# A third row slot lends its place to a head's weights while the expert lookups of a layer begin

## The reference, cut to what matters

```
q   = (xt @ w_q).reshape(T, 8, 2, 128)              # T = 256 tokens, 8 heads
sc  = einsum('thcd,hckd->thck', q, sub_keys)        # scores on 2 x 128 keys per head
...                                                 # two top-16, their sums, a top-16 of those
idx, gate = 16 experts of each head, softmax(top_s)
hid = gelu(einsum('tkd,td->tk', u[idx], x))         # 128 experts of each token
out = einsum('tk,tkd->td', gate * hid, v[idx])
h   = h + out
g   = sigmoid(rms_norm_2(h, ple_norm[i]) @ ple_gate[i])
h   = h + g * (p[i] @ ple_proj[i])
```

## Time and profile before

| | |
|---|---|
| median of three runs | 2379.18 us |
| the profiled execution, its own time | 2381.23 us |
| its span, from the first to the last instruction | 2379.1 us |
| gathers of the first PEER layer, first and last issue | 765.2 and 1415.9 us |
| PE, DVE, ACT, POOL busy | 88%, 73%, 33%, 27% |
| moved by the 16 DMA engines | 726.83 MB, mean 306 GB/s |

### The profile page before, as it was taken

The page is one execution under the profiler, slowest core; times in us unless marked ns, Lnnn a source line. Parts: engine busy times, 40 slices in busy tenths (PEclk is TensorE's granted clock), DMA queues, the critical chain, the costliest instruction groups (busy, mean ns, idle before and its releaser), DMA issues. The chain is left out here.

```text
span 2379.1 us, 26606 instructions
## 1 busy us (share of the span) xinstructions
PE 2101.1 (88%) x9124; PEld 1362.4 (57%) x9124; DVE 1741.4 (73%) x3737; ACT 788.2 (33%) x1479; POOL 633.5 (27%) x520
## 2 busy tenths in 40 slices
PE   8999999999999989887877778999898987777777
PEld 8998889989877544432322226988554532222224
DVE  6555764557766888888787876656888887878786
ACT  4334653346574221211211116344322121211114
POOL 0000000000101444444544440000454554444440
PEclk9999999999999999999999999999999999999999
DMA  7554325554326999999999995535999999999994
GB/s 264 182 183 170 142 103 181 184 187 154 140 89 236 402 420 420 419 419 419 392 420 420 418 391 207 206 142 197 359 419 420 419 419 420 402 420 419 405 420 192
DMA packets 101354, 726.83 MB, mean 306 GB/s; under 512 B 11632, under 2 KB 11888, under 8 KB 13424
## 3 DMA queue, kind: packets, MB, share of 16 engines
q0 software_dynamic: 74016, 539.00, 55.1%
q1 hardware_dynamic: 25200, 181.41, 20.9%
q10 hardware_dynamic: 2016, 4.89, 0.6%
HBM read 724.21 MB, written 1.05 MB: 305 GB/s over the span
## 5 line engine op out<-in xcount | busy, mean ns | idle before, releaser
L2074 PE MATMUL bank<-arena 128*128 128x512 f32 (+4 forms) x2416 | 1072.4, 575 | 235.2 <-DVE arena L1953 230.1
L725 POOL DMA_INDIRECT arena<-in_uv,expert x512 | 622.7, 1216 | 1015.0 <-PE bank L2074 552.3
L2074 PEld LDWEIGHTS bank<-arena 128*128 128x128 f32 (+2 forms) x2416 | 411.6, 193 | 806.0 <-DVE arena L1953 526.2
L2003 DVE SCALAR_TENSOR_TENSOR arena<-arena,xn 128x1024 f32<-128x1024 f32 x512 | 625.9, 1222 | 103.6 <-DMA arena<-in_uv,expert 100.8
L1321 DVE TENSOR_TENSOR lw_rounded<-lw,w_hi 128x2048 fp32r<-128x2048 f32 x153 | 352.8, 2307 | 200.4 <-ACT w_hi L778 197.3
L1216 ACT ACTIVATE act_h<-hid 128x1 f32<-128x1 f32 x512 | 103.8, 203 | 1052.3 <-DVE arena L2003 1051.9
L2074 PE MATMUL bank<-xT_hi,w_hi 128*128 128x256 f32 x1320 | 413.2, 313 | 6.6 <-DVE xT_lo L1366 4.9
L778 ACT ACTIVATE w_hi<-lw 128x2048 fp32r<-128x2048 f32 (+1 forms) x173 | 313.0, 1816 | 237.9 <-PE bank L2074 226.8
L2074 PE MATMUL bank<-xT_lo,w_hi 128*128 128x256 f32 x1320 | 373.5, 283 | 0.0
L2074 PE MATMUL bank<-xT_hi,lw_rounded 128*128 128x256 f32 x1256 | 355.6, 283 | 0.0
L1953 DVE TENSOR_SCALAR arena<-consts,act_h,weight 128x128 f32<-128x128 f32 x512 | 191.2, 373 | 127.0 <-ACT act_h L1216 119.3
(11 more groups left out here) (262 smaller groups left out, 1583.9 us busy)
## 6 DMA issues: line engine op xcount, KB each, us to landing
lw<-in_units SPq DMA_DIRECT2D x165, 1024.0 KB, 4.8
arena<-in_uv,expert POOLq DMA_INDIRECT x512, 14.0
arena<-in_units SPq DMA_DIRECT2D x4, 1024.0 KB, 8.0
wide<-in_wide POOLq DMA_DIRECT2D x2, 1024.0 KB, 8.9
gain<-in_gains ACTq DMA_DIRECT2D x4, 512.0 KB, 9.0
wide<-in_units SPq DMA_DIRECT2D x2, 1024.0 KB, 7.2
h<-in_x SPq DMA_DIRECT2D x2, 512.0 KB, 4.6
arena<-in_ret_consts ACTq DMA_DIRECT2D x1, 1024.0 KB, 4.8
```

Source lines behind the costliest of these rows:

```text
L725: nc.gpsimd.indirect_dma_start(out=rows_uv[:, slot, :], out_offset=None, in_=table, in_offset=bass.IndirectOffsetOnAxis(ap=expert[par][:, ...
L2003: V.scalar_tensor_tensor(rows_uv[:, slot, 0:D], rows_uv[:, slot, 0:D], 1.0, xn[:, tile, :], ALU.mult, ALU.mult, accum_out=hid[par][:, k:k ...
L2074: return nc.tensor.matmul(o, lhsT, rhs, start=start, stop=stop, **more)
```

## The change

Three blocks instead of two hold a head's weights at first: head 4's unit, `head + 5`, goes to a third block of `rows_uv` (block 2 in the first layer, 6 in the second), and that block joins as a slot at gather 43. A layer starts with five slots, has six from gather 16, seven from 29 and eight from 43. The ring's place that held `head + 5` is free for `head + 9`, the projection's unit, which is now loaded right behind `head + 2` and the third block, and no longer after head 4. The third block is loaded behind the wait for `head - 2`, since in the second layer other data lies there before.

```
-UNIT_BLOCKS = ((0, 1), (4, 5))
-JOINS_AT = (16, 29)
+UNIT_BLOCKS = ((0, 1, 2), (4, 5, 6))
+JOINS_AT = (16, 29, 43)
...
-        block_loaded = [sem(f"block_loaded{i}") for i in range(2)]
+        block_loaded = [sem(f"block_loaded{i}") for i in range(len(JOINS_AT))]
...
+                def load_block(i):
+                    sp.dma_start(rows_uv[:, UNIT_BLOCKS[layer][i], :], units_d[head + 3 + i]).then_inc(block_loaded[i], 16)
+
                 for i in range(2):
-                    sp.dma_start(rows_uv[:, UNIT_BLOCKS[layer][i], :], units_d[head + 3 + i]).then_inc(block_loaded[i], 16)
-
-                for u, before in ((head + 2, head - 2), (head + 5, head - 3), (head + 7, head - 1), (head + 6, head + 2), (head + 8, head + 1),
-                                  (head + 9, head + 5)):
+                    load_block(i)
+
+                for u, before in ((head + 2, head - 2), (head + 9, head - 3), (head + 7, head - 1), (head + 6, head + 2), (head + 8, head + 1)):
                     sp.wait_ge(lw_used, before + 1)
                     load_unit(u, u % RING)
+                    if u == head + 2:
+
+                        load_block(2)
```

More of the change, by code:

```diff
@@ L207 @@
         FILLED[layer].append(fills[block])
-BLOCK_OF = {first + 3 + i: UNIT_BLOCKS[layer][i] for layer, first in enumerate((A_PEER0, A_PEER1)) for i in range(2)}
+BLOCK_OF = {first + 3 + i: UNIT_BLOCKS[layer][i] for layer, first in enumerate((A_PEER0, A_PEER1)) for i in range(len(JOINS_AT))}
 LOADS = {u: sum(v not in WHOLE and v not in BLOCK_OF for v in range(u % RING, u + 1, RING)) for u in range(UNITS)}
```

## The result

The changed kernel takes 2382.81 us (median of 20 runs, 2379.91 to 2387.80) against 2378.96 us of the kernel before in the same series. The ratio of the runs is 1.0019, 95% interval [1.0013, 1.0026]: 4.5 us slower. The prediction had +0.6 us, "the same" at 0.87, and a range up to 2383.0. The time lies in the range, and the loss is under the 4.8 us that the prediction called the same. But the interval of ±1.5 us tells it from no change: a small, real loss was forecast as nearly nothing. Two later series of the same kernel gave 1.0010 and 1.0008; weighted by their intervals the three give 1.0014 [1.0009, 1.0018], or +3.3 us, and that is the number to be explained.

The account below looks back on a forecast made before the run. Bounds: an idle gap, a start paced by DVE, PE and slot release, then a long stretch of DMA bytes. First layer 0.0 plus second +0.7, taken as +0.6 on 2379.18, gave 2379.8 us; range 2376.6 to 2383.0.

Parts of the forecast that it names:

- The projection's unit leaves the full stretch: Moving this 1 MB load out of the DMA-bound part, behind gather 36, saves 2.50 us a layer, 5.0 in all.
- the gap: About 5 us before a layer's first gather, DMA share 0.04 in the first; claimed to hide the moved load free.
- rival D: The moved load runs past the first gather, costing up to 2.5 us a layer: 2384.8 us at most; chance 0.03.
- Five slots instead of six for gathers 5 to 15: At each layer's start, late landings delay gather 15: +2.1 to +2.6 us in the first layer, +3.2 in the second.
- the walk: Gathers 5 to 15 followed slot by slot, issue plus latency (7.5 or 8.1 us) against old dots, giving gather 15's delay.
- Gather 5: no cost: First layer's start: issued at 784.12, landing at 791.6, while its dot stood behind others until 792.9 anyway.
- Six slots in place of seven ... cost nothing: Gathers 16 to 28, likewise seven for eight up to 42: queueing covers the lost slot, by 0.2 us at its thinnest.
- The signs: Profile checks: SP's sends, gather issues, DVE waits, about 350 GB/s, gather 17's dot 2 to 3 us later; DMA gaps refute.
- B: The start absorbs the lost slot and the full gain of 5.0 us arrives: 2374.2 us; chance 0.05.
- C: Five and also six slots starve at gathers 8 to 28: +3.5 us a layer, 2386.2 us; chance 0.07.
- The price of the Trainium skill: Fixed 2.0 us plus bytes over 436 GB/s: 4.4 us a gather, making five slots ample, 2374.2 us; prediction rejected it.

Follow-up runs that it names:

- small_proj: Kernel before, loading only 64 of 2048 columns of the projection's unit: 2375.02 us, ratio 0.9983.
- slots_only: Changed kernel, but with the projection's unit loaded last, at its old place behind head 4: 2387.21 us, ratio 1.0033.
- again: The changed kernel, unchanged, timed and profiled once more: 2381.10 us, ratio 1.0010 to the kernel before.
- again2: The changed kernel, unchanged, in a third series and profile: 2380.50 us, ratio 1.0008 to the kernel before.
- gelu_first_after: Changed kernel with ACT's copy of head 1's queries moved behind the gelu of gather 0: 2380.77 us, ratio 1.0003 to the kernel before.
- joins_early: Changed kernel with the lent blocks joining at gathers 14, 27 and 40 instead of 16, 29 and 43: 2381.91 us, ratio 1.0011 to the kernel before.
- null_sem: Kernel before with one more semaphore allocated and never used: 2380.20 us, ratio 0.9999.

## Why the prediction was wrong

- **"The projection's unit leaves the full stretch", −2.50 us a layer: held.** Measured −2.1 to −2.5 us between gathers 36 and 38 in both layers of all three profiles of the changed kernel, −4.0 us [−6.2, −2.1] in small_proj, and −4.5 us between slots_only and the changed kernel. It fits the gap (rival D falls: 0.60 of 5 us, and the first gather lands 6.2 us after its issue, in the kernel before 6.5).
- **"Five slots instead of six for gathers 5 to 15", +2.1 to +2.6 and +3.2 us, 5.3 to 5.8 together: the mechanism held, the term was mis-sized.** This is the step that failed. In the timed runs it is 6.4 us [4.0, 8.6] alone, and 7.9 us [5.0, 10.7] with the six and seven slots behind it; the changed kernel's +3.3 plus the unit's 4.0 (small_proj) to 5.0 (the largest steps) makes 7.3 to 8.3. By the profiles with five slots and no other edit to the start (the first five lines of the table) gather 16 is later by 3.5 us in the first layer (1.5 to 4.8) and 2.9 us in the second (1.4 to 4.5). So by the profiles the first layer's term was about 1 us too small, and the second's right within its spread; together 6.4 us, or 7 to 8 by the runs of the whole change, where the sum had 5.3 to 5.8 and set the full 5.0 against them.
- **Where the size came from.** I put one latency, 7.5 us, through the walk. That row has the same figure as minimum, median and maximum because it counts only one of the four gathers: by their landing events they took 6.9, 7.8, 7.5 and 7.5 us. The 8.1 of the earlier trace rows is one of eight too, which took 8.1 to 8.7. The walk's issues came out right: gather 15 was to go out 45.8 us behind the first gather of the first layer, and went out 46.0, 44.9 and 46.2 us behind it in the three profiles of the changed kernel. But then it took 8.6, 7.9 and 9.7 us to land, not 7.5; before the change it had taken 8.3. The latency isn't a constant: gathers 5 to 15 took 8.7 and 8.5 us in the mean (the two layers) in the first profile, 7.6 and 7.2 in again, 7.8 and 7.8 in again2. The walk also gives every gather the same latency. With six slots gathers 8 to 13 landed 1.3 to 3.2 us before their dots in the first layer and 0.7 to 2.6 in the second, and one that came late used up that lead; with five most have none, and it passes to all that follow. In again2 the dots of gathers 12 to 15 stand so:

```profile
811.71 1.22 DVE L2008 SCALAR_TENSOR_TENSOR arena<-arena,xn 128x1024 f32<-128x1024 f32 x1
...
814.46 1.22 DVE L2008 SCALAR_TENSOR_TENSOR arena<-arena,xn 128x1024 f32<-128x1024 f32 x1 [0.68 <-DMA arena<-in_uv,expert]
...
818.37 1.23 DVE L2008 SCALAR_TENSOR_TENSOR arena<-arena,xn 128x1024 f32<-128x1024 f32 x1 [1.82 <-DMA arena<-in_uv,expert]
...
820.86 1.22 DVE L2008 SCALAR_TENSOR_TENSOR arena<-arena,xn 128x1024 f32<-128x1024 f32 x1 [0.41 <-DMA arena<-in_uv,expert]
```

  Gathers 13 and 14 landed 3.8 and 3.9 us behind the one before each, where 2.5 is the full pace, and 2.4 us of shift came from these two alone. The prediction priced half a microsecond of latency at 1 us, and gave the upper end of that as +2.7 us in all; the measured +3.3 is just beyond it.
- **"Gather 5: no cost": held by the dots of again2, not by the first profile**, where gather 5 landed at 795.50 and its dot started at 795.52. There DVE also waited 1.43 us for gather 7.
- **"Six slots in place of seven ... cost nothing": mostly held.** From gather 16 to 36 the shift changed by −1.0 to +0.1 us in all profiles of the changed kernel but the first, whose first layer lost 2.2 us. There the clock was 0.77 from 848 to 863 us, at 381 GB/s, against 1.00 and 419 in the same place of before. The queue was thin enough then to run empty: gathers 31 and 32 landed 7.8 us after their issue, as quickly as gathers of the start. gelu_first_after had the lower clock in the same place, lost 1.1 us between gathers 31 and 34 of its first layer, and the two gathers took 7.9 and 7.6 us; again2, and again with 0.90 from 844 to 859 us, lost nothing there. Against the clock as the only cause, joins_early lost 1.6 us in that place of its second layer at a clock of 1.00.
- **The signs.** Right: four units within 756.22 to 759.36 (4.0 us later than foreseen, like all of this execution), none near 868, the waits of DVE from the start on, the dot of gather 17 at 3.2 us later (2 to 3 were foreseen) and 4.5 in the second layer; the dot of gather 16 comes 3.2 us later, not under 1. 364 GB/s, not 350. The sign of being wrong, gaps after 816 us, came in the first layer of the first profile, as the dip from 848 to 880 us; again and again2 had 417 to 419 GB/s there. Wrong: the shift was to be gone by gather 45, and was +3.0 / +1.7 in the first profile, −1.9 / −0.9 and +1.1 / +0.2 in the others. The last gather went out at 1421.39, of which 3.96 us are the late start; the other 1.5 us are over the 1 us foreseen.
- **The rivals.** B (the start absorbs it) falls: no profile with five slots has less than 1.4 us at gather 16. C needed more than about 8.8 us of latency and six slots that starve; single gathers of the start took between 6.2 and 9.9 us, but their mean was 7.2 to 8.7 in every profile with five slots, and in the changed kernel no shift grew by more than 0.5 us between gathers 16 and 28: it falls. The price of the Trainium skill, page "DMA: Bandwidth & Descriptors", section "Anatomy of one DMA — SWDGE (gpsimd) path", 4.4 us by estimate, falls with B: the quickest of gathers 5 to 15 took 6.2 us with five slots and 5.4 with four.

What stays open: the profiles of the changed kernel put it at +0.2 us over both layers in their mean (+2.9, −3.4, +1.1), the runs at +3.3 us. Three executions that spread over 6 us don't contradict that, and the trace of before, from which they count, is one execution too: its own time was 2.05 us over the median of its runs, and null_sem stands at −1.3 against it. Which part of the missing 2 to 3 us belongs to the start and which to gathers 16 to 42 isn't settled.

## What to carry to other kernels

A buffer that is lent out at the start of a stream is paid for while the stream is bound by the way round of a slot, not while it is bound by bytes: so shorten that phase, or make up for it with bytes taken out later. Price such a start with the spread of the latency, not with its median, since with the last spare slot goes the lead that hid the late ones: here the first slot taken away cost 6 to 8 us and the second 12. Look how many transfers a latency was read from, too: here it was one. And where two edits of opposite sign nearly cancel, 4 to 8 us each here, forecast the uncertainty of the larger one as the uncertainty of the sum: a chance of 0.87 for less than 4.8 us either way was more than its terms allowed.

## What the runs showed of the hardware

- The first of a gather's sixteen landing events comes at a steady 5.9 to 6.5 us after the issue (mean of gathers 5 to 15, in the five kernels' starts at the head of the table); the last comes 1.2 to 2.6 us behind it in the mean, and this second part makes nearly all the difference between executions: 2.6 and 2.2 us in the first profile of the changed kernel, 1.5 and 1.2 in again. In the full stretch with eight slots it is 5 to 6 us, of 14.7 us from issue to landing.
- In the full stretch landings follow each other at 2.49 us, but one in 17 to 20 comes 0.9 to 1.2 us later than that. Behind gather 60 the fourteen traces have 261 such steps, and each has a transfer of 8 KB in an instruction queue (q14) at most 3.6 us ahead of it. Not every transfer of q14 makes a step (there are 434), and of 140 transfers of 16 KB in the other instruction queue (q8) with none of q14 within 5 us of them not one does.
- TensorE's clock goes to its lower level (1.2 of 2.4 GHz) for some stretches, at places that differ between executions of the same program. One that starts 1 to 3 us behind a layer's first gather (a granted clock of 0.51 from 766.2 to 769.6 us in again2, 1.00 from 769 to 774 us in the first profile) is in 14 of the 20 layers of the ten kernels that leave ACT's order alone, both layers of the kernel before among them. In these the first gather that has to wait for a slot goes out 18.8 to 19.0 us behind the layer's first, in the other six 17.4 to 17.5. At gather 16 it can't be told any more: with five slots the shift there is 1.5 to 3.3 us without such a stretch and 1.4 to 4.8 with it.
